# Full-array products in the recurrence of a gated delta rule (Trainium2, one core)

## The reference, cut to what matters

```python
N = T // CHUNK                      # 512 // 64 = 8 chunks
def step(S, inp):                   # S: 128 x 128 for each head
    qi, ki, ui, wi, ai, gci = inp   # 64 rows each; ai is 64 x 64
    v_new = ui - wi @ S                                             # 64 x 128
    o = (qi * exp(gci)[:, None]) @ S + ai @ v_new                   # 64 x 128
    glast = gci[-1]
    S = S * exp(glast) + (ki * exp(glast - gci)[:, None]).T @ v_new # 128 x 128
    return S, o
```

## Time and profile before

| | |
|---|---|
| time, median of 3 runs | 3062.45 us (3062.33 to 3063.33) |
| profiled execution, span from first to last instruction | 3062.9 us |
| TensorE matmul busy | 2929.8 us, 96% |
| TensorE weight load busy | 2336.1 us, 76% |
| VectorE busy | 1464.3 us, 48% |
| ScalarE busy | 1097.9 us, 36% |
| mean granted TensorE clock of the core | 0.979 |
| recurrence, 283.0 to 354.6 us: mean granted clock | 0.81 |

### The profile page before, as it was taken

How to read it: one execution, slowest core, us unless ns; L and a number is a source line. 1 busy time by engine, 2 the same in 40 slices (tenths; PEclk the granted TensorE clock), 3 DMA queues, 4 the chain that set the end, 5 groups by cost and what they waited for, 6 DMA issues and landing times.

```text
span 3062.9 us, 36220 instructions
## 1 busy us (share of the span) xinstructions
PE 2929.8 (96%) x13458; PEld 2336.1 (76%) x13458; DVE 1464.3 (48%) x2040; ACT 1097.9 (36%) x1784; POOL 224.2 (7%) x166
## 2 busy tenths in 40 slices
PE   8878999989999999999999999999999999999998
PEld 5667777768778888667778888888886677788887
DVE  5653257744344433555454443544434555454432
ACT  4512234433242222555443322333223655432321
POOL 0000000000010012100220002200022000120011
PEclk9998899989999999999999999999999999999999
DMA  3100121103332233111212232222323111222232
GB/s 121 62 14 8 66 83 56 54 29 96 110 101 98 97 104 129 36 44 42 67 58 96 97 105 96 87 96 96 108 90 109 33 51 35 69 89 96 96 107 78
DMA packets 68364, 238.06 MB, mean 78 GB/s; under 512 B 10273, under 2 KB 12449, under 8 KB 67617
## 3 DMA queue, kind: packets, MB, share of 16 engines
q1 hardware_dynamic: 66240, 227.87, 22.5%
q10 hardware_dynamic: 2016, 8.77, 0.8%
HBM read 234.51 MB, written 2.10 MB: 77 GB/s over the span
## 4 chain that ended last, share of the span: by engine, by line
PE 66%; DVE 3%; ACT 2%; issue 1%; DMA 0%; DVEq 0%; ACTq 0%
PE bank L374 18%; PE bank L376 18%; PE bank L375 18%; PE bank L847 3%; PE bank L873 3%; PE bank L653 2%; PE bank L859 2%; PE bank L626 1%; DVE L_scores L965 0%; ACT L_probs L917 0%; PE bank L1460 0%; DMA L_weight_ring<-w_latent 0%; PE bank L226 0%; PE bank L1403 0%; DVE L_area L1781 0%
## 5 line engine op out<-in xcount | busy, mean ns | idle before, releaser
L374 PE MATMUL bank<-L_h_hi,L_w_hi 128*128 128x512 f32 x1776 | 704.5, 397 | 13.6 <-DVE L_weight_ring_low L368 9.6
L376 PE MATMUL bank<-L_h_hi,L_weight_ring_low 128*128 128x512 f32 x1776 | 693.1, 390 | 0.0
L375 PE MATMUL bank<-L_h_lo,L_w_hi 128*128 128x512 f32 x1776 | 692.7, 390 | 0.0
L362 ACT CAST L_w_hi<-L_weight_ring 128x1024 fp32r<-128x1024 f32 (+2 forms) x292 | 326.1, 1117 | 909.1 <-PE bank L376 896.9
L368 DVE TENSOR_TENSOR L_weight_ring_low<-L_weight_ring,L_w_hi 128x1024 fp32r<-128x1024 f32 (+2 forms) x292 | 394.9, 1353 | 378.9 <-ACT L_w_hi L362 378.8
L374 PEld LDWEIGHTS bank<-L_h_hi,L_w_hi 128*128 128x128 f32 x1776 | 334.5, 188 | 90.3 <-issue 15.2
L375 PEld LDWEIGHTS bank<-L_h_lo,L_w_hi 128*128 128x128 f32 x1776 | 334.6, 188 | 74.2 <-issue 5.7
L376 PEld LDWEIGHTS bank<-L_h_hi,L_weight_ring_low 128*128 128x128 f32 x1776 | 334.3, 188 | 70.5
L374 PE MATMUL bank<-L_act_hi,L_w_hi 128*128 128x512 f32 x704 | 273.9, 389 | 0.0
L375 PE MATMUL bank<-L_act_lo,L_w_hi 128*128 128x512 f32 x704 | 273.9, 389 | 0.0
L376 PE MATMUL bank<-L_act_hi,L_weight_ring_low 128*128 128x512 f32 x704 | 273.9, 389 | 0.0
(11 more groups left out here) (317 smaller groups left out, 3796.1 us busy)
## 6 DMA issues: line engine op xcount, KB each, us to landing
L_weight_ring<-ffn_in SPq DMA_DIRECT2D x176, 512.0 KB, 3.2
L_weight_ring<-ffn_out SPq DMA_DIRECT2D x64, 704.0 KB, 4.0
B_weight_ring<-w_sqk SPq DMA_DIRECT2D x24, 512.0 KB, 3.2
B_weight_ring<-w_dn SPq DMA_DIRECT2D x16, 512.0 KB, 3.3
B_weight_ring<-w_gate SPq DMA_DIRECT2D x16, 512.0 KB, 3.2
L_weight_ring<-w_sna_qk SPq DMA_DIRECT2D x16, 512.0 KB, 3.3
L_weight_ring<-w_mix_out SPq DMA_DIRECT2D x16, 512.0 KB, 3.3
B_weight_ring<-w_sv SPq DMA_DIRECT2D x12, 512.0 KB, 3.3
```

The lines of the kernel that those rows point to most:

```text
L362: e.copy(hv.high(at)[:, 0:width], sh.ring[:, at % RING, 0:width]).then_inc(hv.w_hi_done, 1)
L374: e.matmul(out, a_hi, b_hi, start=start, stop=False)
L375: e.matmul(out, a_hi, b_lo, start=False, stop=False)
L376: return e.matmul(out, a_lo, b_hi, start=False, stop=stop)
```

## The change

All products of the recurrence contract 128 rows and write 128 rows of PSUM, where they write rows of tokens at all.

- vn multiplies `w` of the whole tile (128 columns of `LT`) by the state and writes all 128 rows of the bank; VectorE still reads only the 64 rows `R`.
- ks contracts all 128 rows of `kd` and `vnew`. The chunk's new values fill the half `R` of their slot, and the other half of the slot is zero. Even chunks use slot 0 and its first half, odd chunks slot 1 and its second half, so the zero halves are never written again.
- The second product of o contracts all 128 rows of `vnew` and `aT` in the same way. It still writes 64 columns, and the queries' product is as before.
- VectorE clears the two halves once, ahead of the loop, with two memsets of 64 x 512; TensorE and VectorE wait for 3 counts of `zero_s`, not 1.

```diff
-                e.wait_ge(zero_s, 1)
+                e.wait_ge(zero_s, 3)
                 for ck in range(T // CHUNK):
                     t, r = ck // 2, CHUNK * (ck % 2)
-                    R = slice(r, r + CHUNK)
...
                     for h in range(NH):
-                        mm = e.matmul(bank[R, hd(h)], LT[:, t, h * P + r:h * P + r + CHUNK],
-                                      state[:, ck % 2, hd(h)], start=True, stop=True)
+                        mm = e.matmul(bank[:, hd(h)], LT[:, t, hd(h)], state[:, ck % 2, hd(h)], start=True,
+                                      stop=True)
...
                     for h in range(NH):
-                        mm = e.matmul(bank[:, hd(h)], kd[R, t, hd(h)], vnew[R, ck % 2, hd(h)], start=True, stop=True)
+                        mm = e.matmul(bank[:, hd(h)], kd[:, t, hd(h)], vnew[:, ck % 2, hd(h)], start=True, stop=True)
...
-                        mm = e.matmul(bank[:, cols], vnew[R, ck % 2, hd(h)], aT[R, t, h * P + r:h * P + r + CHUNK],
+                        mm = e.matmul(bank[:, cols], vnew[:, ck % 2, hd(h)], aT[:, t, h * P + r:h * P + r + CHUNK],
                                       start=False, stop=True)
...
                 e.memset(state[:, 0, :], 0.0).then_inc(zero_s, 1)
-                e.wait_ge(zero_s, 1)
+                for half in range(2):
+                    e.memset(vnew[(1 - half) * CHUNK:(2 - half) * CHUNK, half, :], 0.0).then_inc(zero_s, 1)
+                e.wait_ge(zero_s, 3)
```

## The result

The changed kernel takes 3036.84 us (median of 4 runs, 3036.27 to 3045.34), the kernel before 3062.89 us beside it. The ratio is 0.9926, with a 95% interval of 0.9914 to 0.9938: faster by 0.6 to 0.9%. Two later measurements, on two different chips, gave 3036.87 and 3036.88 us for the changed kernel, at ratios of 0.9923 and 0.9927. The prediction was 3039.0 us.

What follows compares the result with a forecast made beforehand. TensorE's chain was taken to bound the kernel; shorter recurrence products and a full clock take 23.5 us off 3062.9, giving 3039.4 in the profiled execution and 3039.0 us as the median, range 3034 to 3049.

Steps and rivals of the forecast that it cites:

- o: Output products of each chunk: 16 full-row matmuls take 1.68 us instead of 2.90, saving 9.8 us over 8 chunks.
- ks: State-update products of each chunk: 0.93 us instead of 1.09, saving 1.3 us over 8 chunks.
- vn: Products opening each chunk: 0.88 us instead of 1.02, saving 0.14 in each of six chunks with values.
- First values: Products between vn and ks in six chunks: untouched, 2.95 us stays; at most 0.1 each possible, none counted.
- Chunks 0 and 2: Chunks without values: the 2.05 us from vn to ks stays, each chunk takes 4.66 us, state update hidden.
- The sum: Whole recurrence at full clock: 48.0 us instead of 71.5, so 23.5 us go.
- The clock: TensorE's granted clock in the recurrence: 1.00 throughout instead of 0.81, worth 11.7 of the 23.5 us.
- not idle time: Claim that clock falls in the recurrence follow half-array stretches and o's slow pitch, not TensorE's idle time; no separate size.
- The memsets: Two more VectorE clears before the loop, 0.48 us each, hidden while TensorE is busy: no cost.
- After the loop: TensorE's wait and later stages shift unchanged; 2.2 us allowed for the low end, 1.5 either way for later stages.
- Rival 2: In o: the clock comes back but the slow pitch stays, as operand alternation causes it; gain 11.7 us, 3051; chance 0.03.

Runs made afterwards that it cites:

- e2: Changed kernel with only o's second product contracting 128 rows, vn and ks at 64 rows as before the change: 3046.94 us, ratio 0.9957.
- e3: Kernel before, with o's products reordered: four of the state first, then four of the new values, shapes unchanged: 3050.01 us, ratio 0.9964.
- e9: Changed kernel with only o's second product back at 64 contracted rows, vn and ks full: 3052.31 us in one run.
- e10: Changed kernel with o's products grouped, four of the state then four of the new values, all 128 rows: 3037.43 us in one run.
- e4: Changed kernel with vn as before (64 rows written, 64-column weight loads), ks and o contracting 128 rows: 3038.59 us, ratio 0.9925.
- e5: Changed kernel with first values of tiles 2 and 3 all in odd chunks, so four even chunks are bare: 3038.61 us, one run.
- e6: Kernel before with first values of tiles 2 and 3 all in odd chunks, so four even chunks are bare: 3066.94 us, one run.

## Why the prediction was right

The mechanism was right and so were most terms. One part of the argument on the clock was too strong.

- **o** was put at 16 x 0.105 = 1.68 us and took 1.73. The gain per chunk was 1.17, not 1.22. That the change of rows costs, not the operands' alternation or the 64-row product, is shown by e2, e3, e9 and e10 together.
- **ks** was put at 0.93 and took 0.89 in the chunks with values and 0.96 in the two others; **vn** at 0.88 and took 0.86.
- **First values** were put at 2.95 unchanged and took 2.82. The passage from the values into ks had been a change of rows too. The prediction saw it (at most 0.1 in each of six chunks, taken at nothing). In e4, where vn is as before and ks and o are full, the values take 2.86, so of the 0.13 gained 0.09 belongs to that passage and 0.04 to the one out of vn, which the prediction had not counted.
- **Chunks 0 and 2** were put at 4.66 us each and took 4.85 (282.67 to 287.52) and 4.77. The wait of 2.05 became 2.02 and 2.08. In chunk 0 the state was late: VectorE's update began 0.65 us after o, not the 0.16 of the earlier trace rows, and ended only 0.10 before vn began. The trace, VectorE's steps of chunk 0 and the start of the next vn:

```profile
286.30 1.12 DVE L2761 SCALAR_TENSOR_TENSOR B_job_squares<-B_job_squares,B_arena,bank 128x128 f32<-128x128 f32 x4 [1.76 <-PE bank L2354]
287.52 1.13 PE L2346 MATMUL bank<-B_job_squares,B_arena 128*128 128x128 f32 x8
```

  Elsewhere it begins 0.26 us after o (297.16 against 296.90 in chunk 2) and stays hidden, with some 0.25 us to spare. o can hardly shrink further without meeting it.
- **The sum** was 48.0 us and is 47.70. It is closer than its terms: the values and ks came out lower, chunks 0 and 2 higher.
- **The clock** was forecast at 1.00 throughout, from the comparison in the earlier trace rows, and it was. That full-array products get over the waits of the loop at full clock, where the products of the kernel before don't, is shown by e5 and e6, which have the same waits. In between lies e2, with half-array vn and ks: its clock fell behind chunk 0 and not behind chunk 2. The prediction's "not idle time" goes too far. In e6 more waits cost more, in e3 the only falls in the loop come right behind waits, and in the changed kernel the clock falls behind the wait of 2.81 us after the loop. The slow pitch of o has a share of its own (e3 against the kernel before). Which property of the products the clock follows, the rows used or the work done in a given time, no run here isolates. How much it is worth can be split off: at full clock the six chunks with values gained 7.96 - 6.30 = 1.66 each, 10.0, and the two others 6.04 - 4.85 and 6.04 - 4.77, 2.5. So the products gave 12.5 us and the clock the other 23.86 - 12.5 = 11.4. The forecast was 11.8 and 11.7.
- **The memsets** cost nothing: the last one ended at 281.78, and TensorE went from L2335 into vn at 282.67 without a wait.
- **After the loop** the wait of 2.8 us moved along unchanged, as forecast. The rest was taken as unchanged with 1.5 us either way; three traces of it span 10.6 us. This term of the range was mis-sized. The forecast is 2.2 us above the median, well inside what these stages do by themselves; which of them gave it can't be told from the one trace of the kernel before.
- **Rival 2** had a wrong price. With the clock back and only o's gain missing, 23.5 - 9.8 = 13.7 us would go and not 11.7, which gives 3049 and not 3051, the edge of the range. The trace speaks against it either way: the pitch of o did fall.

## What to carry to other kernels

Small products that use half of the contracted rows are not cheaper than full ones, and next to full ones they are dearer: a stretch that alternates between the two pays at every change, and the clock may fall on top. If zeros for the other half can be had once, outside the loop, fill the array. If they can't, put products with the same row count side by side: that order alone gave 10.9 us here (e3). Where a loop is short beside the kernel, judge the edit by the length and the mean clock of the loop in the trace, because half clock elsewhere moved the total by up to 10.6 us here.

## What the hardware showed that I had not expected

- An effect of what is written, not only of what is contracted: with vn's output at 64 rows and all else full (e4), a chunk took 0.30 us more, of which vn's own start-to-start time (1.02 against 0.86) explains about half; the rest is in the values behind it and in the end of o before it.
- The same 1.04 of 2.00 us of matmul busy time was followed by half clock with half-array products and by full clock with full-array ones. The difference holds although half of the rows of `vnew` that ks and o's second product contract are zeros.
- The clock fell with TensorE busy all of the time (2.00 of 2.00 us in the kernel before, at 327 us) where 128-row and 64-row products alternated, and stayed at 1.00 for 30 us when the same products were grouped (e3).
- The version with bare chunks (e6) made the kernel before slower, at a mean clock of 0.74 in the loop, by moving independent work from four chunks into two without adding any.
